# Key sums in pairs two blocks later, constants behind the input, two weight blocks split early, branch orders rewritten

## What is computed

```
def _layer(x, state, p):
    f = _swiglu(_rmsnorm(x, p['ffn1_norm_pre']), ...)          # D_FF = 2816
    x = x + 0.5 * _rmsnorm(f, p['ffn1_norm_post'])
    m, new_state = _token_mixer(_rmsnorm(x, p['mix_norm_pre']), ...)
    x = x + _rmsnorm(m, p['mix_norm_post'])
    f = _swiglu(_rmsnorm(x, p['ffn2_norm_pre']), ...)
    x = x + 0.5 * _rmsnorm(f, p['ffn2_norm_post'])

def _token_mixer(h, ...):
    proj = h @ p['w_in']                   # split into the three branches and the gates
    qkv, _ = _causal_conv(gdn_qkv, ...)    # 4 taps, SiLU; then q, k = _l2norm(q), _l2norm(k)
    o_gdn = gated delta rule over chunks, _rmsnorm, * silu(z)
    gk = log_sigmoid(gla_r @ gate_up + gate_bias) / 16
    o_gla = gated linear attention over chunks, _rmsnorm, * silu(g)
    o_ssd = state-space scan over chunks (after its own conv), * silu(z), _rmsnorm
    merged = sum over branches of sigmoid(gate) * (o_b @ w_br_b)
    return merged @ p['w_out']
```

## Time and profile before

| what | value |
|---|---|
| median of 3 runs | 3433.2 us (3428.75 to 3434.03) |
| profiled execution: its time, and its span | 3432.56 us, 3430.5 us |
| PE busy | 3235.5 us, 94% of the span |
| DVE, ACT, POOL busy | 1289.8, 770.2, 1569.7 us |
| DMA | 261.10 MB, mean 76 GB/s |
| mean granted clock of PE | 0.969 of full speed |

### The profile page before, as it was taken

The page is one execution under the profiler, slowest core; times in us unless marked ns, Lnnn a source line. Parts: engine busy times, 40 slices in busy tenths (PEclk is TensorE's granted clock), DMA queues, the critical chain, the costliest instruction groups (busy, mean ns, idle before and its releaser), DMA issues. The chain is left out here.

```text
span 3430.5 us, 67730 instructions
## 1 busy us (share of the span) xinstructions
PE 3235.5 (94%) x27178; PEld 3118.5 (91%) x27178; DVE 1289.8 (38%) x2011; ACT 770.2 (22%) x1439; POOL 1569.7 (46%) x948
## 2 busy tenths in 40 slices
PE   7999988999989998999989999889988899899997
PEld 7999988987769998999989999889877799899997
DVE  3331065637752214331043310746477522233301
ACT  2111033323341112111021110333244311221100
POOL 4655544620016654655545655546100266545553
PEclk9999999999979999999999999999999799999999
DMA  3222221200042221222222222212002322212221
GB/s 126 86 86 86 68 77 68 87 31 2 19 146 88 88 88 68 86 86 86 80 72 90 87 84 71 77 68 86 19 2 71 114 88 92 90 62 86 88 83 65
DMA packets 78302, 261.10 MB, mean 76 GB/s; under 512 B 8608, under 2 KB 10656, under 8 KB 77344
## 3 DMA queue, kind: packets, MB, share of 16 engines
q1 hardware_dynamic: 77824, 257.82, 22.7%
q10 hardware_dynamic: 288, 0.49, 0.1%
HBM read 243.70 MB, written 14.58 MB: 75 GB/s over the span
## 5 line engine op out<-in xcount | busy, mean ns | idle before, releaser
L539 POOL TENSOR_SCALAR wh<-raw 128x1024 fp32r<-128x1024 f32 (+1 forms) x464 | 470.6, 1014 | 1763.5 <-PE ps L580 1216.7
L541 POOL TENSOR_TENSOR wl<-raw,wh 128x1024 fp32r<-128x1024 f32 (+1 forms) x464 | 1065.4, 2296 | 67.8 <-POOL wh L539 0.3
L576 PE MATMUL ps<-hh,wh 128*128 128x272 f32 x4768 | 1003.8, 292 | 67.8 <-DVE hl L1865 44.5
L578 PE MATMUL ps<-hl,wh 128*128 128x272 f32 x4768 | 994.0, 290 | 0.0
L580 PE MATMUL ps<-hh,wl 128*128 128x272 f32 x4768 | 989.0, 289 | 0.0
L576 PEld LDWEIGHTS ps<-hh,wh 128*128 128x128 f32 x4768 | 757.6, 190 | 77.5 <-issue 59.1
L578 PEld LDWEIGHTS ps<-hl,wh 128*128 128x128 f32 x4768 | 754.2, 190 | 0.0
L580 PEld LDWEIGHTS ps<-hh,wl 128*128 128x128 f32 x4768 | 753.6, 189 | 0.0
L576 PE MATMUL ps<-ah,wh 128*128 128x272 f32 x1408 | 294.5, 291 | 0.0
L578 PE MATMUL ps<-al,wh 128*128 128x272 f32 x1408 | 290.3, 287 | 0.0
L1874 DVE SCALAR_TENSOR_TENSOR f<-f,prm,rstd_post 128x544 f32<-128x544 f32 x48 | 43.7, 916 | 653.7 <-ACT rstd_post L1352 653.7
(11 more groups left out here) (429 smaller groups left out, 3657.5 us busy)
## 6 DMA issues: line engine op xcount, KB each, us to landing
raw<-in_up SPq DMA_DIRECT2D x176, 512.0 KB, 3.2
raw<-in_win SPq DMA_DIRECT2D x80, 512.0 KB, 3.2
raw<-in_merge SPq DMA_DIRECT2D x96, 384.0 KB, 3.0
raw<-in_down SPq DMA_DIRECT2D x64, 512.0 KB, 3.5
raw<-in_down SPq DMA_DIRECT2D x32, 384.0 KB, 3.1
raw<-in_wout SPq DMA_DIRECT2D x16, 512.0 KB, 3.2
states<-in_in_gdn SPq DMA_DIRECT2D x2, 2048.0 KB, 8.3
proj<-in_in_ssd SPq DMA_DIRECT2D x2, 2048.0 KB, 8.5
```

The lines of the kernel that those rows point to most:

```text
L539: pool.tensor_scalar(hi, src, 1.0, 1.0, MULT, MULT).then_inc(hi_done, 1)
L541: pool.tensor_tensor(lo, src, hi.bitcast(F32), SUB).then_inc(lo_done, 1)
L576: pe.matmul(out, high, mh_[:, c], start=a, stop=False)
L578: pe.matmul(out, high, ml_[:, c], start=False, stop=False)
```

## The change

It does five things. (1) At the start, SP loads `wpre`, the tail of the constants (from `ONES` on, 186 KB), two of the eight input tiles, weight block 0, the other six input tiles, weight blocks 1 to 3, and then the rest of the constants and `prm`. PE, ACT and DVE wait for the first two (`first_in`, 32), ACT also for the input part, DVE for the rest only after its eight `hl`; the ACT table is loaded before the wait. (2) Key sums come in pairs after windows 12 + 2, 4, 6 and 8, so that the sums of tiles t and t + 1 follow window 12 + t + 2. (3) In the second feed-forward part, blocks 2 and 3 are split before blocks 0 and 1, as soon as the merge is over. (4) The three orders are replaced; among PE's 194 pieces that are not empty, the mean piece moves by 0.6 places and the farthest by 6. (5) The division of the GLA gate by 16 is taken out of DVE (one operation for each of five steps) and put into the scale of ACT's evictions. Two semaphores are shared.

```diff
+KEY_BLOCKS = (2, 4, 6, 8)
...
-    "shlgslgnlssglsglgnglgnhlglglglglgnlglglgnlgnnhhnlglgngslnlnghnslggnlglglglhsglgsslglslglglglngll"
+    "slngslggsshhsllghglgnglglgnlsnglglglglglhnglngnlglnglglgnnlggslgnlgglslgglsnlhslslglnglgnsnhlhgl"
...
+FIRST_ORDER = (0, 1, 2, 3), (2, 3, 0, 1)
+def split_count(which, j):
+    return FIRST_ORDER[which].index(j) + 1
...
-            sp_.dma_start(cst[:], io["cst"]).then_inc(loaded, 16)
-            sp_.dma_start(x[:], io["x"].rearrange("p (k t) -> p k t", k=KD)).then_inc(loaded, 16)
-            sp_.dma_start(wpre[:], ...).then_inc(loaded, 16)
+            sp_.dma_start(wpre[:], ...).then_inc(first_in, 16)
+            sp_.dma_start(cst[:, ONES:NCONST], io["cst"][:, ONES:NCONST]).then_inc(first_in, 16)
...
+                if layer == 0:
+                    load_x(0, slice(0, 2))
+                    ups(layer, 0, B_FFN1, 0, slice(0, 1))
+                    load_x(1, slice(2, KD))
+                    ups(layer, 0, B_FFN1, 0, slice(1, 4))
+                    sp_.dma_start(cst[:, 0:ONES], io["cst"][:, 0:ONES]).then_inc(loaded, 16)
...
+            def first_blocks(layer, which, first):          # POOL
+                for j in FIRST_ORDER[which]:
...
+                    pool.wait_ge(raw_full[j], ...)
+                    if which and j >= SPLIT:
+                        pool.wait_ge(blk_done, layer * BLOCKS + B_OUT + SPLIT)
+                    else:
+                        pool.wait_ge(blk_done, layer * BLOCKS + first + min(j + 1, SPLIT))
+                    pool.tensor_scalar(hi, src, 1.0, 1.0, MULT, MULT).then_inc(hi_done, 1)
...
-            def key_sums(layer, t):
-                slot = (t + 2) % 4
+            def key_sums(layer, block, second):
+                slot, t = (block + 2 + second) % 4, block - 2 + second
                 pe.wait_ge(key_["sq"], layer * KEYS + t + 1)
-                pe.wait_ge(evict_done, layer * 40 + 12 + t + 3)
+                pe.wait_ge(evict_done, layer * 40 + 12 + block + 3 + second)
...
-                for t in range(KEYS + 2):
-                    if t >= 2:
-                        pe.wait_ge(key_["ln"], layer * KEYS + t - 1)
+                for t in range(KEYS + 4):
+                    if t - 2 in KEY_BLOCKS or t - 3 in KEY_BLOCKS:
+                        pe.wait_ge(key_["ln"], layer * KEYS + t - 3)
                     window(3 + t // 4, t % 4)
-                    if t < KEYS:
-                        key_sums(layer, t)
+                    if t in KEY_BLOCKS:
+                        for second in range(2):
+                            key_sums(layer, t, second)
...
-            act.wait_ge(loaded, 48)
             act.preload_act_table_set(LN_EXP)
+            act.wait_ge(first_in, 32)
...
+                def roots(block):                            # ACT
+                    for t in (block - 2, block - 1):
+                        act.wait_ge(key_["ss"], layer * KEYS + t + 1)
+                        act.activation(... ACT.Ln, bias=epsc).then_inc(key_["ln"], 1)
+                    for t in (block - 2, block - 1):
+                        act.wait_ge(key_["ln"], layer * KEYS + t + 1)
+                        act.activation(... ACT.Exp, scale=-0.5).then_inc(key_["rs"], 1)
...
+                for t in range(8):
                     block_in(0, 3, t)
                     act.activation(halves(proj[:, LQ + t, :]), pair(t % 4), ACT.Copy).then_inc(evict_done, 1)
+                    if t in KEY_BLOCKS:
+                        roots(t)
+                        for k in (t, t + 1):
+                            square(k)
+                roots(KEY_BLOCKS[-1])
...
-                dve.tensor_scalar(L["gk"][0:n, :], L["gk"][0:n, :], 1.0 / GLA_NORMALIZER, None, MULT).then_inc(l_["gk"], 1)
...
-                dve.wait_ge(prm_in, value(dve, layer * 16 + 16))
                 if layer == 0:
                     for k in range(KD):
                         scaled_low(0, 0, k)
+                    dve.wait_ge(loaded, 16)
+                dve.wait_ge(prm_in, value(dve, layer * 16 + 16))
```

More of the change, by code:

```diff
@@ L353, in halves @@
             return ap.rearrange("p (a t) -> p a t", a=2)
-        started = sem("started")
-        loaded = sem("loaded")
+        loaded, first_in = sem("loaded"), sem("first_in")
+        x_in = [sem(f"x_in{i}") for i in range(2)]
         prm_in = sem("prm_in")
@@ L404, in value @@
                 eng.compute_val(v)
-                eng.wait_ge(started, 1)
+                eng.wait_ge(first_in, 32)
             return v
@@ L431, in tiles, with ups @@
                 return io[name][bass.ds(index, 1)].rearrange("a p (k m) -> p (a k) m", m=P)
-            def ups(layer, which, first, i):
-                blocks(layer, first, i, (KD,) * 4, lambda j: tiles("up", layer * (2 * UPS) + i * 4 + (which * UPS + j)))
+            def ups(layer, which, first, i, part=slice(None)):
+                blocks(layer, first, i, (KD,) * 4, lambda j: tiles("up", layer * (2 * UPS) + i * 4 + (which * UPS + j)), part)
             def ffn(layer, which, first):
-                with sp_.Fori(1, KF // 2) as i:
+                if which:
+                    for j in range(4):
+                        sp_.wait_ge(lo_done, layer * BLOCKS + first + split_count(which, j) + RAW)
+                        ups(layer, which, first, 1, slice(j, j + 1))
+                with sp_.Fori(2 if which else 1, KF // 2) as i:
                     ups(layer, which, first, i)
@@ L541, in blocks, with ffn @@
                     pool.tensor_tensor(lo, src, hi.bitcast(F32), SUB).then_inc(lo_done, 1)
-            def ffn(layer, first):
-                blocks(layer, first, 0, (KD,) * 4, ahead=True)
+            def ffn(layer, which, first):
+                first_blocks(layer, which, first)
                 with pool.Fori(1, KF // 2) as i:
@@ L550, in _ @@
             for layer in range(DEPTH):
-                ffn(layer, B_FFN1)
+                ffn(layer, 0, B_FFN1)
                 blocks(layer, B_PROJ, 0, (2,) * 4)
@@ L558, in _ @@
                     blocks(layer, B_OUT, i, (KD,) * 4)
-                ffn(layer, B_FFN2)
+                ffn(layer, 1, B_FFN2)
         @block.tensor
         def _(pe):
-            pe.wait_ge(loaded, 48)
+            pe.wait_ge(first_in, 32)
             def products(j, slot, ks, moving, start, stop, ready=None, ahead=False):
@@ L659, in first_blocks @@
                             if k == 0:
-                                pe.wait_ge(lo_done, value(pe, layer * BLOCKS + first + j + 1 + RAW))
+                                pe.wait_ge(lo_done, layer * BLOCKS + first + split_count(which, j) + RAW)
                             last = products(j, j, (k,), lambda n: h_tiles(k), k == 0, k == KD - 1, ahead=True)
@@ L1260, in _ @@
                 ffn(layer, 0, B_FFN1)
+                if layer == 0:
+                    pe.wait_ge(loaded, 16)
                 pre_stats(layer, 2)
@@ L1523, in gla @@
                     act.activation(L["dl"][:, a:a + m, :].rearrange("p l t -> p (l t)"),
-                                   ps[:, 4:6, :].rearrange("p b c -> p (b c)")[:, 0:m * 256], ACT.Exp).then_inc(l_["d2"], 1)
+                                   ps[:, 4:6, :].rearrange("p b c -> p (b c)")[:, 0:m * 256], ACT.Exp,
+                                   scale=1.0 / GLA_NORMALIZER).then_inc(l_["d2"], 1)
                     yield
@@ L1835, in _ @@
             dve.memset(cb[:, 0:1], 0.0).then_inc(s_["yc"], 1)
-            dve.memset(cb[:, 1:2], 0.0).then_inc(started, 1)
-            dve.wait_ge(loaded, 48)
+            dve.wait_ge(first_in, 32)
             def scale(k, wcol):
@@ L2498, in _ @@
                         if r:
-                            last.then_inc(mac_tmp, 1)
-                            dve.wait_ge(mac_tmp, value(dve, layer * 16 + i * 4 + (2 * k + r)))
+                            last.then_inc(own, 1)
+                            dve.wait_ge(own, layer * (5 * KD) + KD + i * 4 + (2 * k + r))
                             last = dve.tensor_tensor(mac[:, k, :], mac[:, k, :], mt_[:, 0, :], ADD)
```

71 lines of the change are left out of this document (37 added, 34 removed).

## The result

The changed kernel takes 3413.7 us (median of 5 runs, 3412.05 to 3418.69) against 3433.2 us (3428.75 to 3438.39): a ratio of 0.9941, 95% interval 0.9929 to 0.9952. It is 19.5 us faster. The forecast was 3397, its range 3383 to 3411: the direction was right, the gain about half of what was forecast, and the time lies outside the range by 2.7 us. The profiled execution took 3413.56 us, span 3411.5.

A forecast was written before the change was run, and what follows sets the result against it. PE, busy 94% of the span, was taken as the bound, so only shortening its gaps or its work gains: 3432.6 - 9.7 - 16.0 - 6.8 - 4.0 = 3396.1, with 0.6 for the median 3397 us; 8 in 10 from 3383 to 3411.

The forecast's parts named there:

- The start: Start of the kernel: with the first loads reordered, PE starts at 9.9 us instead of 19.67; 9.7 us gain taken.
- The order and the releaser: At the start: first input part lands before weight block 0, and POOL's `wl` releases PE's first matmul at about 10 us.
- The key sums: PE's wait for ACT's squares in each layer: gap 5.2 us in place of 13.5; 8.0 us a layer, 16.0 in all.
- on top of the last convolution tile: Key-sum gap: POOL's split now falls on DVE's last convolution tile and moves everything by 2.5 to 2.6 us.
- the chain leads by 1.9 us: After the key sums: ACT and DVE's chain to the eviction window 32 needs gains 1.9 us on its old times.
- the eviction chain binds: Rival, chance 0.12: chain keeps its old times and PE stalls at window 32; 5.8 us a layer, 3401 us in all.
- Early splits: Head of feed-forward part two: blocks 2 and 3 split in earlier pauses, PE starts sooner; 3.4 us twice, 6.8.
- Branches and orders: Branches stage: gate division taken out of DVE and new orders gain 2 us a layer, 4 in all.
- no wide error at all: The forecast itself holding, 3397 us with its own range 3391 to 3403, rather than any rival; chance 0.56.

The follow-up runs named there:

- s_wpre: Changed kernel with the small 8 KB transfer of norm weights issued behind weight block 0 instead of first; 3415.5 us, a single run.

## Why the prediction was wrong

- **The start, 9.7 forecast, 6.5 measured (7.3 on average: 60.2 us to split 6 in the two kernels with the old start, 52.9 in the others of the table).** The order and the releaser were right. The step that failed is that the amount ahead of a transfer, read off the GB/s of the kernel before, gives its landing time: block 0 was forecast for 6.2 and landed at 7.8. The queue had moved 0.5 MB less at 5.4 us. The small transfer issued first is part of the reason (0.7 of the 1.6 us by s_wpre, one profile); the rest is not settled. The split took 0.4 more beside DVE's first `hl`. The speed of the first sums took 1.4 in the two traces compared and about 0.2 on average.
- **The key sums, 16.0 forecast, 5.0 measured (4.9 + 4.1 - 4.0).** Two steps failed. The first is "on top of the last convolution tile": the split of window 15's block also fell on the tile before it, which the gap had kept free of it, so the convolution moved by 5.9 us and not by 2.6, and PE's gap was 8.5 and not 5.2. A copy of three columns waited 2.2 us there, until POOL's operation ended to within 0.03 us. The Trainium skill's page "SBUF — State Buffer", section "SBUF: two separate sides", which the prediction weighed against this term, says that one of the two engines has the port pair for a whole instruction, and it counts an fp32 copy in SBUF among the operations of DVE that take the pair. The trace agrees. By that rule the forecast would have gone the right way, but it too was applied to one tile only. The second is "the chain leads by 1.9 us". That lead was worked out from a gain of 8.3 at the gap; with 4.9 and 4.1 the chain came later than PE instead. The last key root ended 6.5 us earlier in layer 1 (613.4 before, 606.9 after), where PE's lead at the gap had been 7.9, and 18.7 earlier in layer 2 (2318.0, 2299.3), where it had been 20.9. And the length of the chain was taken as fixed, where the meeting with POOL makes it 37.3 or 41.8 us. The eviction that window 28 needs was about 9.0 us ahead of it before and still 3.2 in layer 1 (644.3 against 647.5); in layer 2 it was 7.2 before and came 2.0 too late. So the rival *the eviction chain binds* came true in one layer of two, as it does in 12 of 20, and took back 3.8 us, at another window than forecast; it was given 0.12. At window 32, the place forecast, PE waits 0.5 us at most.
- **Early splits, 6.8 forecast.** Right in mechanism and size: the wait of PE at part two of layer 2 is 5.2 us in place of 8.3, and the stages show 3.3 and 3.0. In the two traces compared alone it seemed 2.8 and 2.4. What is missing to 3.4 in layer 2 is that POOL's last split still ran 0.6 us into DVE's first `normed`, which took 1.21 us and not 0.88.
- **Branches and orders, 4 forecast.** 1.8 a layer on average, in keeping with the forecast, but not told from nothing. The wait for the sample states was not shortened but moved (21.1 us over both layers at L612, none at L938).
- **The bounds.** The range took its lower gains from one rival at a time. Start and key sums were short together, by 13.4 us; the chance of "no wide error at all", 0.56, was too high for a sum of four terms of which two rest on how two engines meet.

The stages add up to 7.3 + 5.0 + 6.3 + 3.6 = 22.2 us. The 2.7 us to the 19.5 measured are not traced to one place. In the two traces compared, 0.7 were lost in windows 22 to 37 of layer 1 (100.5 us against 99.8), where window 28 did not stall, and chance at the start, at the head of the projection and in the branches is of that size.

## What to carry to other kernels

When a gap of one engine is closed, look at what the others did in its shelter: here POOL's splits had stood still for 18.8 us, and the critical DVE work ran undisturbed because of it. Where POOL and DVE share a stretch and only one of them is urgent, let the other wait for it on a semaphore: that gave 14 us here for one wait instruction (3413.7 to 3399.9 us in two groups of runs; 13.6 by the stages). Compute the slack of a buffer chain for its first user and for both ways in which two engines can meet, not for one trace's.

## What the runs showed of the hardware that was not expected

- The same 48 matmuls of a block take between 5.97 and 6.06 us. The value stays to within 0.01 for ten and more blocks and changes only at a wait of PE. In layer 2's projection the kernel before had 5.97 throughout and the changed one 6.05 before the gap, 6.00 behind it and 5.97 behind the stall; over such a stage that is 1 to 2 us which no instruction explains. Here it took 1.0 us of lead (splits 308 to 322) in the windows ahead of the layer 2 gap.
- Two engines meeting within 0.06 us, with one or the other first, made a difference of 4.5 us 38 us later, and up to 3.8 us of the kernel's time; the order of the two told the stall in 20 layers of 20.
- The same stage at the head of the projection takes 10.1 to 10.4 or 11.9 to 12.0 us, and the granted clock there is 1.00 or 0.50 to 0.60, in any of the kernels; in the three stages looked at closer, one fast and two slow, the wait ahead of it was the same 1.3 us.
- The same first sums at the start took between 1.75 and 2.02 us, and the next between 1.08 and 2.02, in different kernels and executions, while the granted clock reads 1.00 there. Four records in 2.02 us is the pace of the eight in 3.97 at a granted clock of 0.50, so the low clock is the likely reason, but no row shows it. What sets this stays open.
